# A hybrid decoder trunk on one core: the last up unit of a feed-forward window, made in two halves of 256 columns

## The chip, the cores and the metric

The kernel runs on one core of one Trainium2 chip. The metric is device time in microseconds (us) of one execution. Three runs of the kernel before took 2665.16, 2666.79 and 2670.24 us, so the median is 2666.79.

The engines are named as in the profile: PE (TensorE matmuls), PEld (its weight loads), DVE (VectorE), ACT (ScalarE), POOL (GpSimd) and SP (SyncE, which issues the DMAs). Each runs its own program in order, and they wait for each other through semaphores.

## The reference

The input x has 1024 tokens of 1024 features, in float32. Two layers follow each other, then a last RMSNorm. In each layer

```python
h = rmsnorm(x, norm_mix[l])
proj = h @ w_in[l]
mix = concat([s5_mixer(...), dsa_attention(...), retention(...)])   # all causal
x = x + mix @ w_out[l]
h = rmsnorm(x, norm_ffn[l])
gate, up = jnp.split(h @ w_ffn_in[l], 2, axis=-1)      # 2816 columns each
x = x + (jax.nn.silu(gate) * up) @ w_ffn_out[l]
```

The change lies in the last three lines, the feed-forward part.

## The kernel before, in words

**Tiling.** Features lie on the 128 partitions, tokens on the free axis. The tokens are worked through in two halves of 512 (h = 0, 1) in each of the two layers (l = 0, 1). A *unit* is one product of a 128-feature slice of weights with all of the input features for 512 tokens: 8 feature tiles of 128. Its result fills one PSUM bank of 512 columns. There are 408 units, numbered u in the order in which they run. They are grouped in *windows*: `proj` (18 units), `mixout` (8) and `ffn` (76).

**Three products for one.** To keep float32 accuracy with the faster float32r products, each operand is split into a rounded high part and the low remainder. A tile product is then hi x hi + hi x lo + lo x hi, so a unit of 8 tiles has 24 products of 512 columns on PE, first the 16 with the weights' high part, then the 8 with their low part.

**Weights.** For unit u SP loads the slice into `w_raw` (three buffers) when unit u - 3 is done. ACT makes `w_hi` from it (`prep`, L835; two buffers, so it waits until unit u - 2 is done), POOL makes `w_lo` as the difference (`weight_lo`, L724).

**The feed-forward window.** The 22 slices of gate and up come in four chunks (4, 6, 6 and 6), listed in `FFN`: in a chunk gate and up units alternate, then eight down units multiply the chunk's 4 or 6 activation tiles with `w_ffn_out` and DVE adds them to x (`add_x`, L1179). Behind each chunk but the last, the first gate unit of the next chunk stands between the last up unit and the first down unit. In the last chunk the last up unit (number 67 of the window) stands directly ahead of the first down unit (number 68).

**From an up unit to an activation tile.** DVE multiplies the unit's bank with the gate (`atmp`, L1319). ACT rounds the product to `a_hi` (L942), and POOL makes the remainder `a_lo` (L806). A down unit needs both. In its first unit PE begins with all tiles of the chunk but the last (two products for each of five tiles here), then waits on `a_lo_ready` for the last.

**The order on ACT and POOL.** At the step of a unit, ACT's program first has `prep` of the unit behind it and then the `a_hi` of the up unit before it; POOL's has `weight_lo` of the unit behind it and then `a_lo`. So at the first down unit ACT's order is: cast of the weights of the second down unit (which waits for the end of the up unit), then `a_hi`; POOL's is: `w_lo` of the second down unit (which waits for that cast), then `a_lo`.

**Banks.** PSUM has eight banks of 512 columns: A and B are used by the units in turn, C and D (two each), E and F by the mixers. Before PE writes into a bank it calls `take`, which waits for the semaphore that `leave` noted when the bank was last filled: that of the engine which reads it out.

**The order of everything** is one list, `PLAN`, which each engine walks through. The mixers' steps are woven between the units. The attention of the half that comes next runs inside an `ffn` window: layer l, half 1 in the window (l, 0), and layer 1, half 0 in the window (0, 1); the window (1, 1) has none. The attention ends with `attend_end`. In its step 0 PE fills bank E with the last block's values (and leaves it to `mat_ready`) and bank F with the row factors; then ACT copies F (L1040), and in step 1 DVE reads E and writes the block's output (`block_out`, L1381), which counts `mat_ready` up. In the windows (0, 0) and (1, 0) the plan has both steps between the gate unit 66 and the up unit 67; in the window (0, 1) step 0 stands ahead of unit 66 and step 1 behind it.

Of the kernel before, what the change touches and what calls it, by code (L numbers as in the profile page):

```python
# [10 lines left out]
ALU = mybir.AluOpType  # L11
ACTF = mybir.ActivationFunctionType
F32 = mybir.dt.float32
# [4 lines left out]
P = 128  # L18
T, D, DEPTH = 1024, 1024, 2
HALF = 512  # L20
KT = D // P
TT = HALF // P
NB = T // P
# [27 lines left out]
FFN = []  # L51
# [225 lines left out]
def deferred(kind, l, h):  # L277

    return (kind, l, h) == ("proj", 1, 1) or kind == "ffn" and (l, h) != (0, 1)
# [4 lines left out]
    return (2, 3, 4, 5, 6, 0, 1, 7) if l else (0, 1, 6, 7, 2, 3, 4, 5)  # L284


def unit_pieces(u):
    kind, _, _, i = UNIT[u]
    return 2 if kind == "proj" and i == U_VK else 1
# [70 lines left out]
def build_trunk(nc, x, w_in, w_out, norm_mix, a_re, a_im, log_dt, b_re, b_im, c_re, c_im, ssm_d, glu_w,  # L360
                glu_b, rel_bias, ret_gn, norm_ffn, w_ffn_in, w_ffn_out, norm_final, const, out, at):
    ctx = ExitStack()
    with ctx:
# [134 lines left out]
        def bank(group, a=0, b=None):  # L498
            first, n = GROUPS[group]
            return psum[:, first * 512 + a:first * 512 + (n * 512 if b is None else b)]  # L500
# [8 lines left out]
        def w_lo(u, n=1024):  # L509
            return low[:, u % 3, 0:n]  # L510
# [14 lines left out]
                 "gate_ready", "atmp_ready", "a_hi_ready", "a_lo_ready", "x_added", "x1_stored", "x_out0",  # L525
                 "x_out1", "x_in0", "x_in1", "xa_loaded", "q_moved", "final_loaded", "final_turned", "final_out",
                 "out_stored0", "out_stored1", "out_stored2", "act_chain", "dve_chain", "pool_chain",
                 "round_step"] + [f"xtok_loaded{t}" for t in range(NB)]
        sems = {n: ctx.enter_context(nc.semaphore(n)) for n in names}
        block = ctx.enter_context(nc.Block())  # L530

# [183 lines left out]
        @block.gpsimd  # L715
        def _(eng):
            st = Counts()

            def weight_lo(u):
                if u >= UNITS:  # L720
                    return
                n = unit_width(u)
                eng.wait_ge(sems["hi_ready"], u + 1)
                eng.tensor_tensor(w_lo(u, n), w_raw[:, u % 3, 0:n], w_hi[:, u % 2, 0:n].bitcast(F32),  # L724
                                  ALU.subtract).then_inc(sems["weights_ready"], 1)

            def tile_lo(k, src):

                n = st.add("h_hi_ready")
                if k % 2 == 0:  # L730
                    eng.wait_ge(sems["h_hi_ready"], n)
                    eng.tensor_tensor(h_lo[:, k, :], src, h_hi[:, k, :].bitcast(F32), ALU.subtract).then_inc(  # L732
                        sems["h_lo_pool"], 1)

            def add_square(m):
                n = st.add("square_ready")
                if 0 < m < KT - 1:
                    eng.wait_ge(sems["square_ready"], n)
                    if m > 1:
                        eng.wait_ge(sems["ssq_added"], st.now("ssq_added"))  # L740
                    eng.tensor_tensor(ssq[:, :], ssq[:, :], tmp[:, 2 + m % 2, :], ALU.add).then_inc(sems["ssq_added"], 1)
                    st.add("ssq_added")

            def masks(l, h, b, j):

                at_ = attention[l, h]
                nk, heads = NK[b], 2 * at_.pairs
                far = nk - 256
                if (l, h, b, j) == (0, 0, 0, 0):
                    eng.wait_ge(sems["const_loaded"], 16)  # L750
                    eng.wait_ge(sems["bias_loaded"], 16)
                    eng.wait_ge(sems["y_gated"], 1)
                    for g in range(2):
                        eng.wait_ge(sems[f"x_out{g}"], 16)
                if b >= 2 and j == 0:
                    eng.wait_ge(sems["mask_ready"], st.add("mask_ready"))
                if st.now("nmax_ready"):
                    eng.wait_ge(sems["nmax_ready"], st.now("nmax_ready"))
                st.add("nmax_ready", heads)
                if b < 2:  # L760
                    for n in range(heads):
                        win = bias_win[:, 2 * j + n, ::-1]
                        if b:
                            eng.tensor_copy(at_.mask(b, n, 0, P), win[:, 0:P])
                        eng.tensor_tensor(at_.mask(b, n, nk - P, nk), table("noncausal"), win[:, P:256], ALU.add).then_inc(
                            sems[f"mask{n % 2}_ready"], 1)
                    return
                if j == 0:
                    eng.tensor_copy(at_.near, score[b][:, far:nk]).then_inc(sems["pool_chain"], 1)
                    for n in range(1, heads):  # L770
                        eng.tensor_copy(at_.mask(b, n, 0, far), score[b][:, 0:far])
                    eng.wait_ge(sems["pool_chain"], st.add("pool_chain"))
                for n in range(heads):
                    eng.tensor_tensor(at_.mask(b, n, far, nk), at_.near, bias_win[:, 2 * j + n, ::-1], ALU.add).then_inc(
                        sems[f"mask{n % 2}_ready"], 1)

            for step in PLAN:
                what = step[0]
                if what == "fillnorm":
                    if step[2:4] == (0, 0):  # L780
                        weight_lo(0)
                    for k in range(KT):
                        tile_lo(k, fill_tmp(step[4], k))
                elif what == "fillraw" and step[2]:
                    st.add("h_hi_ready", KT)
                elif what == "fillmix":
                    for k in mix_order(step[1]):
                        tile_lo(k, mix_source(step[2], k))
                elif what in GEMMS:
                    kind, l, h, i, u = step  # L790
                    if i < GEMMS[kind]:
                        weight_lo(u + 1)
                    if kind == "mixout" and i:
                        add_square(i - 1)
                    if kind == "ffn" and i:
                        did, c, f = FFN[i - 1]
                        if did == "gate" and deferred(kind, l, h):
                            eng.wait_ge(sems["gate_ready"], st.add("gate_ready"))
                            eng.tensor_tensor(gate, gate, row, ALU.mult).then_inc(sems["gate_scaled"], 1)
                        elif did == "gate":  # L800
                            st.add("gate_ready")
                        if did == "up":
                            if (l, h, c, f) == (0, 0, 0, 0):
                                eng.wait_ge(sems["q_moved"], 16)
                            eng.wait_ge(sems["a_hi_ready"], st.add("a_hi_ready"))
                            eng.tensor_tensor(a_lo[:, f, :], atmp, a_hi[:, f, :].bitcast(F32), ALU.subtract).then_inc(  # L806
                                sems["a_lo_ready"], 1)
                        if did == "down" and c == LAST_CHUNK:
                            add_square(f)
                            if h == 0:  # L810
                                tile_lo(f, mix_source(1, f))
                            elif l == 0:
                                st.add("h_hi_ready")
                elif what == "attend":
                    _, l, h, b, j, s = step
                    if s == 0 and j == 0:
                        masks(l, h, b, 0)
                    elif s == 1 and j + step_pairs(l, h) < PAIRS:
                        masks(l, h, b, j + step_pairs(l, h))
# [3 lines left out]
        def _(eng):  # L823
# [100 lines left out]
            def ffn(l, h, i, u):  # L924
# [13 lines left out]
                    act(gate, scaled, ACTF.Silu).then_inc(sems["gate_ready"], 1)  # L938
                if did == "up":
                    st.add("a_lo_ready")  # L940
                    eng.wait_ge(sems["atmp_ready"], st.add("atmp_ready"))
                    act(a_hi[:, f, :], atmp, ACTF.Copy).then_inc(sems["a_hi_ready"], 1)  # L942
                if did == "down":
                    st.add("x_added")
                    if c == LAST_CHUNK:
# [221 lines left out]
        def _(eng):  # L1167
# [131 lines left out]
            def ffn(l, h, i, u):  # L1299
# [7 lines left out]
                        eng.wait_ge(sems["gate_ready"], st.now("gate_ready"))  # L1307
                    tt(scaled, bank(g), row, MUL).then_inc(sems["gated"], 1)  # L1308
                elif did == "up":
                    eng.wait_ge(sems["unit_done"], u)  # L1310
                    st.add("gate_ready")
                    if later:
                        eng.wait_ge(sems["gate_scaled"], st.add("gate_scaled"))
# [2 lines left out]
                    if st.now("a_lo_ready"):  # L1316
                        eng.wait_ge(sems["a_lo_ready"], st.now("a_lo_ready"))
                    st.add("a_lo_ready")
                    tt(atmp, bank(g), gate, MUL).then_inc(sems["atmp_ready"], 1)  # L1319
                elif did == "down":  # L1320
                    eng.wait_ge(sems["unit_done"], u)
                    add_x(f, g)
# [426 lines left out]
        def _(eng):  # L1749
# [11 lines left out]
            def take(*groups):  # L1761

                for g in groups:
                    first, n = GROUPS[g]
                    for b in range(first, first + n):
                        for sem, count in kept.pop(b, ()):
                            eng.wait_ge(sems[sem], count)
# [88 lines left out]
            def ffn(l, h, i, u):  # L1856
# [7 lines left out]
                g = unit_bank("ffn", i)  # L1864
                if what == "gate":
                    unit(g, u, "gated" if deferred("ffn", l, h) else "gate_ready")
                elif what == "up":
                    unit(g, u, "atmp_ready")
                else:
# [381 lines left out]
```

## Time and profile before

| | |
|---|---|
| runs, us | 2665.16, 2666.79, 2670.24 |
| span of the profiled execution, us | 2668.5 |
| time of the profiled execution beside its span | not listed |
| mean granted TensorE clock | 0.987 |
| busy: PE, PEld | 2551.4 us (96%), 2007.8 us (75%) |
| busy: DVE, POOL, ACT | 1553.0 us (58%), 1308.9 us (49%), 1020.3 us (38%) |
| DMA | 232.91 MB, 87 GB/s on average |

The profile shows one execution. A row of a group of instructions gives line, engine, operation, tiles as out<-in, shape and count, then the busy time in us and the mean duration of one in ns, then the engine's idle time before them and what ended it. A row of the timeline gives the start and the length in us, counted from the start of the span, and in brackets the idle time ahead of it and what ended that. The duration of a product runs from its start to its modelled end; products overlap, so their pace is read from their starts.

### The profile page before, as it was taken

The page shows a single profiled execution, that of the slowest core. Times are in us where ns is not written, and L with a number is a line of the kernel's source. Part 1 is how long each engine was busy: PE and PEld are TensorE (multiplying, and loading weights), DVE is VectorE, ACT ScalarE, POOL GpSimd, SP SyncE. Part 2 cuts the span into 40 slices and gives each one's busy share as a digit, 9 for nine tenths or more (in the row PEclk, how much of TensorE's full clock was granted, in tenths as well). Part 3 has the DMA queues.
Part 4 walks back from the last instruction along what each step waited for, and adds up shares of the span by engine and source line. Part 5 has one row for each costly group of instructions (what it writes and reads, how often), then busy time and mean ns, then how long its engine had stood idle before and what let it go on. Part 6 is the DMA issues. An engine that isn't in the chain of part 4 may idle for free.

```text
span 2668.5 us, 34623 instructions
## 1 busy us (share of the span) xinstructions
PE 2551.4 (96%) x13515; PEld 2007.8 (75%) x13515; DVE 1553.0 (58%) x2691; ACT 1020.3 (38%) x1478; POOL 1308.9 (49%) x818
## 2 busy tenths in 40 slices
PE   8998979999999999999999999999999999999998
PEld 6766757677777777778777787777777777888887
DVE  3769767799997226833331385677999922211111
ACT  5232354244435433324344422442534453322222
POOL 3332344455545564536555532544555447665654
PEclk9988999999999999999999999999999999999998
DMA  5341112132222153323322242222222215233332
GB/s 165 85 132 41 49 53 90 52 91 72 78 71 64 58 189 95 87 64 91 91 77 82 80 138 56 79 60 76 77 77 60 79 44 201 79 103 103 108 110 82
DMA packets 385666, 232.91 MB, mean 87 GB/s; under 512 B 29593, under 2 KB 371553, under 8 KB 383073
## 3 DMA queue, kind: packets, MB, share of 16 engines
q1 hardware_dynamic: 385136, 229.62, 29.0%
q8 instruction: 109, 1.79, 0.3%
q10 hardware_dynamic: 368, 1.08, 0.1%
q14 instruction: 53, 0.43, 0.0%
HBM read 213.88 MB, written 14.69 MB: 86 GB/s over the span
## 4 chain that ended last, share of the span: by engine, by line
PE 68%; DVE 25%; ACT 3%; issue 3%; POOL 1%; DMA 1%; DVEq 0%; ACTq 0%; SPq 0%
PE psum L1759 65%; DVE scores L1361 7%; DVE top L1359 7%; PE psum L2079 1%; DVE psum L1395 1%; DVE xs L1179 1%; DVE scores L1347 1%; DVE tmp L1319 1%; ACT w_hi L835 0%; ACT scratch L1036 0%; POOL w_lo L724 0%; DVE tmp L1308 0%; DVE scratch L1428 0%; PE psum L2176 0%; ACT xs L1054 0%
## 5 line engine op out<-in xcount | busy, mean ns | idle before, releaser
L724 POOL TENSOR_TENSOR w_lo<-w_raw,w_hi 128x1024 fp32r<-128x1024 f32 (+2 forms) x408 | 900.8, 2208 | 1197.9 <-ACT w_hi L835 1197.8
L1759 PE MATMUL psum<-h_hi,w_hi 128*128 128x512 f32 x1984 | 796.4, 401 | 15.2 <-ACT h_hi L859 7.4
L835 ACT ACTIVATE w_hi<-w_raw 128x1024 fp32r<-128x1024 f32 (+2 forms) x408 | 397.7, 975 | 1047.9 <-PE psum L1759 989.4
L1759 PE MATMUL psum<-h_lo,w_hi 128*128 128x512 f32 x1984 | 763.2, 391 | 0.9 <-POOL h_lo L732 0.9
L1759 PE MATMUL psum<-h_hi,w_lo 128*128 128x512 f32 x1984 | 514.4, 390 | 0.0
L1759 PEld LDWEIGHTS psum<-h_hi,w_hi 128*128 128x128 f32 x1984 | 374.9, 189 | 128.3 <-issue 36.1
L1759 PEld LDWEIGHTS psum<-h_lo,w_hi 128*128 128x128 f32 x1984 | 373.9, 189 | 78.3 <-issue 1.9
L1759 PEld LDWEIGHTS psum<-h_hi,w_lo 128*128 128x128 f32 x1984 | 373.3, 188 | 76.6
L1359 DVE MAX8 top<-scores 128x8 f32<-128x512 f32 (+5 forms) x352 | 324.3, 921 | 7.8
L1361 DVE MATCH_REPLACE8 scores<-top,scores 128x512 f32<-128x512 f32 (+5 forms) x352 | 319.0, 906 | 0.0
L1179 DVE TENSOR_TENSOR xs<-xs,psum 128x512 f32<-128x512 f32 x160 | 109.6, 686 | 315.0 <-PE psum L1759 304.5
L1759 PE MATMUL psum<-a_hi,w_hi 128*128 128x512 f32 x704 | 279.2, 397 | 7.2 <-POOL a_lo L806 7.2
L1759 PE MATMUL psum<-a_lo,w_hi 128*128 128x512 f32 x704 | 274.9, 390 | 0.0
L1319 DVE TENSOR_TENSOR tmp<-psum,tmp 128x512 f32<-128x512 f32 x88 | 60.8, 691 | 245.0 <-PE psum L1759 243.9
L1759 PE MATMUL psum<-a_hi,w_lo 128*128 128x512 f32 x704 | 182.7, 393 | 0.0
L1759 PEld LDWEIGHTS psum<-a_hi,w_hi 128*128 128x128 f32 x704 | 132.6, 188 | 41.9 <-POOL a_lo L806 8.9
L1759 PEld LDWEIGHTS psum<-a_hi,w_lo 128*128 128x128 f32 x704 | 133.5, 190 | 28.1
L1759 PEld LDWEIGHTS psum<-a_lo,w_hi 128*128 128x128 f32 x704 | 132.7, 188 | 26.5
L806 POOL TENSOR_TENSOR a_lo<-tmp,a_hi 128x512 fp32r<-128x512 f32 x88 | 116.9, 1329 | 30.8 <-ACT a_hi L942 30.8
L1308 DVE TENSOR_TENSOR tmp<-psum,tmp 128x512 f32<-128x512 f32 x66 | 45.6, 691 | 122.1 <-PE psum L1759 114.8
L1759 PE MATMUL psum<-w_hi,h_hi 128*128 128x512 f32 x256 | 102.8, 402 | 4.4 <-ACT iqT L905 4.3
L1759 PE MATMUL psum<-w_hi,h_lo 128*128 128x512 f32 x256 | 100.5, 393 | 0.0
(310 smaller groups left out, 2913.5 us busy)
## 6 DMA issues: line engine op xcount, KB each, us to landing
w_raw<-in_w_ffn_in_dram SPq DMA_DIRECT2D x176, 512.0 KB, 3.8
w_raw<-in_w_ffn_out_dram SPq DMA_DIRECT2D x96, 384.0 KB, 3.1
w_raw<-in_w_in_dram SPq DMA_DIRECT2D x68, 512.0 KB, 3.8
w_raw<-in_w_out_dram SPq DMA_DIRECT2D x32, 512.0 KB, 3.6
x_half<-xs SPq DMA_DIRECT2D x8, 1024.0 KB, 6.5
xs<-x_half SPq DMA_DIRECT2D x8, 1024.0 KB, 6.9
w_raw<-in_w_ffn_out_dram SPq DMA_DIRECT2D x32, 256.0 KB, 2.7
out_dram<-mixed SPq DMA_DIRECT2D x8, 512.0 KB, 4.5
```

Source lines behind the costliest of these rows:

```text
L724: eng.tensor_tensor(w_lo(u, n), w_raw[:, u % 3, 0:n], w_hi[:, u % 2, 0:n].bitcast(F32), ALU.subtract).then_inc(sems["weights_ready"], 1)
L806: eng.tensor_tensor(a_lo[:, f, :], atmp, a_hi[:, f, :].bitcast(F32), ALU.subtract).then_inc(sems["a_lo_ready"], 1)
L835: act(w_hi[:, u % 2, 0:n], w_raw[:, u % 3, 0:n], ACTF.Copy).then_inc(sems["hi_ready"], 1)
L1179: tt(xs[:, m, :], xs[:, m, :], bank(g), ADD).then_inc(sems["x_added"], 1)
L1308: tt(scaled, bank(g), row, MUL).then_inc(sems["gated"], 1)
L1319: tt(atmp, bank(g), gate, MUL).then_inc(sems["atmp_ready"], 1)
L1347: ins = stt(score[b], bank(g, 0, NK[b]), w, score[b], MUL, ADD)
L1359: eng.max(out=top8[:, :], in_=src).then_inc(sems["round_step"], 1)
L1361: eng.match_replace(out=src, in_to_replace=top8[:, :], in_values=src, imm_value=TAKEN).then_inc(sems["round_step"], 1)
L1395: eng.tensor_tensor_reduce(bank(g, 0, nk), bank(g, 0, nk), at_.mask(b, n), -1.0, 3e38, ADD, ALU.min, nmax[:, i:i + 1]).then_inc(sems["nmax ...
L1759: return eng.matmul(out_, lhsT, rhs, start=start, stop=stop, skip_group_check=True)
L2079: ins = eng.transpose(bank(g, k * P, (k + 1) * P), at_.prob[:, n, k * P:(k + 1) * P], ident)
```

## The change

The last up unit of each window is made in two halves of 256 columns. `halved(i)` is true where unit i is an up unit and unit i + 1 a down unit. PE makes columns 0 to 255 in bank E (all 24 products, each of 256 columns), counts `up_half` up, then makes columns 256 to 511 in the unit's own bank and counts `unit_done` up. DVE, ACT and POOL each make their step in two halves, with semaphores `atmp_half` and `a_hi_half` for the first half and the old ones for the second. PE takes both banks before its first product.

```diff
+def halved(i):
+    return 0 < i + 1 < len(FFN) and FFN[i][0] == "up" and FFN[i + 1][0] == "down"
...
 # POOL
+                            if halved(i - 1):
+                                eng.wait_ge(sems["a_hi_half"], st.add("a_hi_half"))
+                                eng.tensor_tensor(a_lo[:, f, 0:256], atmp[:, 0:256], a_hi[:, f, 0:256].bitcast(F32),
+                                                  ALU.subtract)
+                                eng.wait_ge(sems["a_hi_ready"], st.add("a_hi_ready"))
+                                eng.tensor_tensor(a_lo[:, f, 256:512], atmp[:, 256:512],
+                                                  a_hi[:, f, 256:512].bitcast(F32), ALU.subtract).then_inc(
+                                    sems["a_lo_ready"], 1)
...
 # ACT
+                    if halved(i - 1):
+                        eng.wait_ge(sems["atmp_half"], st.add("atmp_half"))
+                        act(a_hi[:, f, 0:256], atmp[:, 0:256], ACTF.Copy).then_inc(sems["a_hi_half"], 1)
+                        eng.wait_ge(sems["atmp_ready"], st.add("atmp_ready"))
+                        act(a_hi[:, f, 256:512], atmp[:, 256:512], ACTF.Copy).then_inc(sems["a_hi_ready"], 1)
...
 # DVE
+                    if halved(i - 1):
+                        eng.wait_ge(sems["up_half"], st.add("up_half"))
+                    else:
+                        eng.wait_ge(sems["unit_done"], u)
...
+                    if halved(i - 1):
+                        tt(atmp[:, 0:256], bank("E", 0, 256), gate[:, 0:256], MUL).then_inc(sems["atmp_half"], 1)
+                        eng.wait_ge(sems["unit_done"], u)
+                        tt(atmp[:, 256:512], bank(g, 256, 512), gate[:, 256:512], MUL).then_inc(sems["atmp_ready"], 1)
...
 # PE
+                elif halved(i):
+                    hi, lo = w_hi[:, u % 2, :], w_lo(u)
+                    eng.wait_ge(sems["hi_ready"], u + 1)
+                    take("E", g)
+                    for c0 in (0, 256):
+                        cols = slice(c0, c0 + 256)
+                        out_ = bank(g if c0 else "E", c0, c0 + 256)
+                        for k in range(KT):
+                            w = slice(k * P, (k + 1) * P)
+                            mm(out_, hi[:, w], h_hi[:, k, cols], k == 0, False)
+                            mm(out_, hi[:, w], h_lo[:, k, cols], False, False)
+                        eng.wait_ge(sems["weights_ready"], u + 1)
+                        for k in range(KT):
+                            ins = mm(out_, lo[:, k * P:(k + 1) * P], h_hi[:, k, cols], False, k == KT - 1)
+                        ins.then_inc(sems["unit_done" if c0 else "up_half"], 1)
+                    leave("E", "atmp_half")
+                    leave(g, "atmp_ready")
```

The semaphores `up_half`, `atmp_half` and `a_hi_half` are new. The other units are made as before.

## Rows read from the trace of the kernel before

**Rows 1.** The page: busy time of each engine; the chain that ended last, by engine.
```profile
PE 2551.4 (96%) x13515; PEld 2007.8 (75%) x13515; DVE 1553.0 (58%) x2691; ACT 1020.3 (38%) x1478; POOL 1308.9 (49%) x818
...
PE 68%; DVE 25%; ACT 3%; issue 3%; POOL 1%; DMA 1%; DVEq 0%; ACTq 0%; SPq 0%
```

**Rows 2.** The waits of PE: engine, line, waited for: us, times, longest us.
```profile
PE psum L1759 <- POOL a_lo L806: 7.2, 4, 1.8
```

**Rows 3.** The timeline around the end of the up unit, window (1, 1).
```profile
2613.51 1.98 PE L1759 MATMUL psum<-h_hi,w_lo 128*128 128x512 f32 x8
2615.33 0.39 PE L1759 MATMUL psum<-a_hi,w_hi 128*128 128x512 f32 x1
2615.53 0.69 DVE L1319 TENSOR_TENSOR tmp<-psum,tmp 128x512 f32<-128x512 f32 x1 [4.75 <-PE psum L1759]
2615.53 0.85 ACT L835 ACTIVATE w_hi<-w_raw 128x768 fp32r<-128x768 f32 x1 [4.07 <-PE psum L1759]
...
2616.28 0.61 ACT L942 ACTIVATE a_hi<-tmp 128x512 fp32r<-128x512 f32 x1
2616.45 1.83 POOL L724 TENSOR_TENSOR w_lo<-w_raw,w_hi 128x768 fp32r<-128x768 f32 x1 [2.35 <-ACT w_hi L835]
...
2617.37 0.39 PE L1759 MATMUL psum<-a_lo,w_hi 128*128 128x512 f32 x1
2618.24 1.26 POOL L806 TENSOR_TENSOR a_lo<-tmp,a_hi 128x512 fp32r<-128x512 f32 x1
2619.55 0.50 PE L1759 MATMUL psum<-a_hi,w_hi 128*128 128x512 f32 x1 [1.80 <-POOL a_lo L806]
```

**Rows 4.** The group of POOL that makes the activations' low parts.
```profile
L806 POOL TENSOR_TENSOR a_lo<-tmp,a_hi 128x512 fp32r<-128x512 f32 x88 | 116.9, 1329 | 30.8 <-ACT a_hi L942 30.8
```

**Rows 5.** The timeline of POOL: a pair of operations on 256 columns.
```profile
1460.01 0.74 POOL L774 TENSOR_TENSOR scores<-scratch,bias_win 128x256 f32<-128x256 f32 x1
1460.70 0.74 POOL L774 TENSOR_TENSOR scratch<-scratch,bias_win 128x256 f32<-128x256 f32 x1
```

**Rows 6.** Groups of DVE and ACT by shape: 256 columns out of PSUM.
```profile
L1447 DVE TENSOR_TENSOR scratch<-psum,cst 128x256 f32<-128x256 f32 x32 | 12.0, 418 | 32.4 <-PE psum L1759 32.4
L1078 ACT ACTIVATE scratch<-psum 128x256 f32<-128x256 f32 x16 | 6.0, 377 | 39.6 <-PE psum L1759 39.6
```

**Rows 7.** Groups of PE by shape: 4-byte products of 512 and 256 columns.
```profile
L1759 PE MATMUL psum<-uy,area 128*128 128x512 f32 x48 | 23.3, 594 | 0.9 <-ACT scratch L1014 0.9
...
L1759 PE MATMUL psum<-uy,area 128*128 128x256 f32 x16 | 4.8, 379 | 0.0
```

**Rows 8.** 128 columns per weight: group of PE, timeline, group of weight loads.
```profile
L1759 PE MATMUL psum<-s_ct,scores 128*128 128x128 f32 x64 | 7.5, 275 | 0.0
...
204.07 3.73 PE L1759 MATMUL psum<-s_ct,scores 128*128 128x128 f32 x32
...
L1759 PEld LDWEIGHTS psum<-h_hi,w_hi 128*128 128x128 f32 x1984 | 374.9, 189 | 128.3 <-issue 36.1 <-ACT h_hi L859 8.4 <-ACT w_hi L835 4.2
```

**Rows 9.** The timeline ahead of the up unit, windows (0, 0) and (0, 1).
```profile
904.37 0.48 PE L1759 MATMUL psum<-h_hi,w_hi 128*128 128x512 f32 x1
904.65 0.60 ACT L1040 ACTIVATE scratch<-psum 128x512 f32<-128x512 f32 x1 [7.89 <-PE psum L1759]
905.28 0.69 DVE L1381 TENSOR_TENSOR mixed<-psum,scratch 128x512 f32<-128x512 f32 x1 [11.13 <-ACT scratch L1040]
...
1486.23 0.69 DVE L1381 TENSOR_TENSOR mixed<-psum,scratch 128x512 f32<-128x512 f32 x1 [2.05 <-ACT scratch L1040]
...
1490.87 0.39 PE L1759 MATMUL psum<-h_hi,w_hi 128*128 128x512 f32 x1
```

**Rows 10.** Stretches from PE's restart to the third down unit, with granted clock.
```profile
914.15:920.22 6.07, 6.07 (x27) 4.99 (x27) 0.69 (x1) 1.89 (x3) 2.97 (x2) 1.00 0.23 67
1500.53:1508.15 7.62, 7.62 (x26) 6.16 (x27) 2.51 (x2) 1.98 (x3) 1.84 (x1) 0.78 0.17 52
2205.03:2211.09 6.06, 6.06 (x26) 4.99 (x27) 0.69 (x1) 1.89 (x3) 2.96 (x2) 1.00 0.23 68
2619.55:2627.19 7.64, 7.64 (x26) 6.13 (x27) 0.69 (x1) 1.36 (x2) 1.84 (x1) 0.78 0.18 54
```

More of the change, by code:

```diff
@@ L527, in build_trunk @@
                  "out_stored0", "out_stored1", "out_stored2", "act_chain", "dve_chain", "pool_chain",
-                 "round_step"] + [f"xtok_loaded{t}" for t in range(NB)]
+                 "round_step", "up_half", "atmp_half", "a_hi_half"] + [f"xtok_loaded{t}" for t in range(NB)]
         sems = {n: ctx.enter_context(nc.semaphore(n)) for n in names}
@@ L804, in _ @@
                                 eng.wait_ge(sems["q_moved"], 16)
-                            eng.wait_ge(sems["a_hi_ready"], st.add("a_hi_ready"))
-                            eng.tensor_tensor(a_lo[:, f, :], atmp, a_hi[:, f, :].bitcast(F32), ALU.subtract).then_inc(
-                                sems["a_lo_ready"], 1)
+                            if halved(i - 1):
[7 more added lines that the diff above has]
+                            else:
+                                eng.wait_ge(sems["a_hi_ready"], st.add("a_hi_ready"))
+                                eng.tensor_tensor(a_lo[:, f, :], atmp, a_hi[:, f, :].bitcast(F32), ALU.subtract).then_inc(
+                                    sems["a_lo_ready"], 1)
                         if did == "down" and c == LAST_CHUNK:
@@ L940, in ffn @@
                     st.add("a_lo_ready")
-                    eng.wait_ge(sems["atmp_ready"], st.add("atmp_ready"))
-                    act(a_hi[:, f, :], atmp, ACTF.Copy).then_inc(sems["a_hi_ready"], 1)
+                    if halved(i - 1):
[3 more added lines that the diff above has]
+                        act(a_hi[:, f, 256:512], atmp[:, 256:512], ACTF.Copy).then_inc(sems["a_hi_ready"], 1)
+                    else:
+                        eng.wait_ge(sems["atmp_ready"], st.add("atmp_ready"))
+                        act(a_hi[:, f, :], atmp, ACTF.Copy).then_inc(sems["a_hi_ready"], 1)
                 if did == "down":
@@ L1309, in ffn @@
                 elif did == "up":
-                    eng.wait_ge(sems["unit_done"], u)
+                    if halved(i - 1):
+                        eng.wait_ge(sems["up_half"], st.add("up_half"))
+                    else:
+                        eng.wait_ge(sems["unit_done"], u)
                     st.add("gate_ready")
@@ L1318, in ffn @@
                     st.add("a_lo_ready")
-                    tt(atmp, bank(g), gate, MUL).then_inc(sems["atmp_ready"], 1)
+                    if halved(i - 1):
+                        tt(atmp[:, 0:256], bank("E", 0, 256), gate[:, 0:256], MUL).then_inc(sems["atmp_half"], 1)
+                        eng.wait_ge(sems["unit_done"], u)
+                        tt(atmp[:, 256:512], bank(g, 256, 512), gate[:, 256:512], MUL).then_inc(sems["atmp_ready"], 1)
+                    else:
+                        tt(atmp, bank(g), gate, MUL).then_inc(sems["atmp_ready"], 1)
                 elif did == "down":
```

## The prediction

> **What bounds the kernel now.** I read the page first: TensorE (PE) is busy for 96% of the span, and in the chain that ended last PE has 68% and VectorE (DVE) 25% [rows 1]. So a microsecond counts if PE stands still for it or spends it on products. Next I read PE's own waits, because the change sits between the last up unit of a feed-forward window and its first down unit: PE waited for POOL's a_lo (L806) 4 times, 7.2 us in all, 1.8 us the longest [rows 2]. Four windows, four waits: that is the place, and 7.2 us is all that stands there.
>
> The timeline of the last of the four shows what ends the wait [rows 3]. The up unit's last products start at 2613.51 (eight in 1.98 us); the first down unit begins at 2615.33 without a gap. The up result is seen by the other engines at 2615.53: DVE multiplies it with the gate (0.69), and ACT begins the cast of the next down unit's weights (L835, 0.85), which waits for the same result and stands ahead of a_hi in ACT's program. a_hi follows at 2616.28 and is done at 2616.89. POOL starts at 2616.45, when the cast ends, with the low part of those weights (L724, 1.83), and only then makes a_lo (2618.24, 1.26, so to 2619.50). PE goes on at 2619.55. The reader is to see that a_hi lay ready for 2618.24 - 2616.89 = 1.35 us before POOL took it up. The late chain is cast, w_lo, a_lo; the product and a_hi are not on it.
>
> **The change, part by part.** It acts on one unit in each of the four windows: only in the last chunk does an up unit stand directly ahead of a down unit.
>
> *The halved chain.* DVE can make its first half once half the unit is done. But ACT's first half of a_hi is still written behind the cast, which waits for the whole unit, and POOL's first half of a_lo behind w_lo, which waits for that cast. Nothing on the late chain starts earlier. The half products and casts are hidden: a DVE operation on 256 columns from PSUM takes 0.42, one of ACT 0.38 [rows 6], so the second product ends by 2615.53 + 0.42 = 2615.95 and two casts from 2616.28 on end by 2617.04, still 1.2 us ahead of POOL. Without that cover, what exceeds 1.2 us would add to the stall. DVE's new wait holds only its own second half and the later additions to x, ACT's comes after the cast and is met by then; behind POOL's waits stands the w_lo of a later unit. SyncE's weight loads wait on the unit's end as before.
>
> What is left is that POOL makes two operations of one. A pair on 256 columns: the second starts 0.69 after the first and takes 0.74, together 1.43 [rows 5], against 1.26 in place [rows 3], hence +0.17 (the mean of all a_lo, 1.33, holds slower ones [rows 4]). From below, halves that cost exactly half add 0; from above, 2 x 0.74 and a pause of 0.07 as between cast and w_lo [rows 3] make 1.55, +0.29. I take the pair, as the nearest row: 4 x 0.17 = +0.7 us (0 to 1.2).
>
> *Half-width products.* 24 products of 512 columns become 48 of 256, each with a weight load of its own. The 512-column pace is (1.98 - 0.39)/7 = 0.227 us [rows 3]. No product in this number format is narrower in the trace, so I bound it. If the pace is proportional to the columns, 256 cost 0.1135 and the unit is unchanged. The 4-byte products at their slower rate fall from 594 to 379 ns between 512 and 256 columns, 0.84 ns a column [rows 7]; half of that is 0.42 for this format, whose 512 columns would be 0.215, which leaves 0.012 fixed per product: 0.107 + 0.012 = 0.119 then, and 48 x 0.119 - 24 x 0.227 = +0.27 us a unit. Above that stands the row of rival B. I take 0.118, nearer the fixed end, because it is what differs between the two formats: +0.22 a unit, +0.9 us in all (0 to 1.1).
>
> Does a weight load hide behind a product this short? Products on 128 columns with a new 128x128 weight each ran 32 in 3.73 us, that is (3.73 - 0.275)/31 = 0.111 apart, though a load is listed with 189 ns [rows 8]: loads overlap with the stream and with one another. So 0.118 isn't held up by them. The Trainium skill (TensorE: Matmul & The Clock Gate, "Measured speedup vs the span model") says instead that a weight load overlaps with running matmuls only where the row group differs, and all loads here use every row. By that rule and the page's figure for a load of 128 columns (section "LDWEIGHTS", about 107 ns) the 24 added loads of a unit would show, an estimate of 2.6 us a unit and 10 us in all. The rows above speak against it.
>
> *A second bank.* This is the largest term. The first half goes to bank E, so PE must now wait, before the unit's first product, for whoever last used E. In the feed-forward windows that carry the attention of a second half (two of four, one in each layer), PE's last attention step stands directly ahead of this very up unit: it fills E (the weighted values) and F, and E is free only when DVE has made the block's output (L1381), which needs ACT's copy of F (L1040). In the trace PE starts the unit at 904.37, while ACT's copy runs from 904.65 and L1381 from 905.28 to 905.97 [rows 9]. With 0.05 from DVE's end to PE's start, as behind a_lo [rows 3], the unit starts at 906.02: +1.65 us. Everything behind it on PE moves by that; nothing takes it back, since the gate's chain ended before the unit did and down products follow. The other such window has the same rows some 1291 us later. In layer 0's second window E is free at 1486.23 + 0.69 = 1486.92 and the unit starts at 1490.87 [rows 9]: no wait. The fourth has no attention. So 2 x 1.65 = +3.3 us (to 3.5 with a weight load of 0.1 shown after each pause).
>
> *The clock.* Two of the four stalls of 1.8 us are followed by the lower level. From PE's restart to the third down unit takes 6.07 and 6.06 us at a granted clock of 1.00, and 7.62 and 7.64 at 0.78, where PE ran partly at 1.2 instead of 2.4 GHz [rows 10]. So a fall costs 1.6 us. A slightly longer stall and two new pauses can bring one more fall, shifted times one fewer; I put 0 into the sum and -1.6 to +3.2 into the range.
>
> **The sum.** 0.7 + 0.9 + 3.3 = +4.9 us. The profiled execution has a span of 2668.5 (no time of its own is listed beside that), 1.7 above the median of the runs, 2666.79. On the span it gives 2673.4; on the median, the figure that will be compared, 2671.7.
>
> **Rivals.**
> A. *Faster: the early half frees the end of POOL's chain.* Place: POOL between the unit's end and a_lo. If the first halves of a_hi and a_lo were done before w_lo, or a_lo were bound by a_hi, the stall would shrink and the clock would hold: at most 4 x 1.8 + 2 x 1.6 = 10.4 gained against 0.9 + 3.3 paid, 6.2 us faster, 2660.6. It decides in favour of the change once each stall is below 1.8 - 4.2/4 = 0.75 us. For it speaks only that the second half is all that needs the end of the unit; against it, that a_hi now waits 1.35 us for POOL [rows 3].
> B. *Weight loads show at half width.* The 24 added loads at the 189 ns listed [rows 8] are 4.5 us a unit, 18.1 in all, and with 0.7 + 3.3 that makes 22 us: 2688.9. For it: no 256-column product of this format has been seen. Against it: 0.111 apart at 128 columns.
> C. *No wait for bank E*, because E is released early enough or PE is late there anyway: 0.7 + 0.9 = +1.6 us, 2668.4. For it: only two instances, and an order of steps that I read from the plan. Against it: 904.37 is 1.6 us before L1381's end.
> D. *The clock falls more often*, twice to three times net: 4.9 + 3.2 to 4.8, 8.1 to 9.7 us: 2674.9 to 2676.5. For it: the two falls after stalls of 1.8 us; against it, the two stalls without one.
> That the change does not do what it says (an early chain that is not early) is already the forecast's first part.
>
> **How the numbers follow.** Forecast 0.64, A 0.05, B 0.07, C 0.12, D 0.12. 0.2% of the median is 5.3 us, about what a measurement of this kernel can tell from no change. The forecast's 4.9 lies just inside, and by its own bounds (0 + 0 + 3.3 to 1.2 + 1.1 + 3.5, and one fall either way) it goes 0.36 to "same" and 0.28 to slower. A goes to faster, C to "same", B and D to slower: faster 0.05, same 0.48, slower 0.47. The range reaches from below C to the upper end of D, 2667.8 to 2677.0, and leaves out A, B and tails.
>
> **What would show it.** PE's four waits for a_lo at 1.9 to 2.1 us, not shorter; the a_lo group with four more operations, eight of them on 256 columns, the first right behind w_lo; 48 products in 5.6 to 5.75 us without gaps; PE idle before the up unit of the first and third windows by 1.4 to 1.7 us, released by DVE L1381. It would be wrong if the a_lo waits fall below 1.5 us, if the half products stand over 0.13 apart, or if no wait for E appears.

## The result: slower by 0.3 to 0.5 per cent

The changed kernel took 2680.55 us in the median of four runs (2679.74 to 2684.52); the kernel before, in four runs, 2665.97. The ratio is 1.0049 with a 95% interval from 1.0034 to 1.0064. Measured again later beside 31 runs of the kernel before, the ratio was 1.0030 (1.0019 to 1.0041), which is 8.0 us (5 to 11) of 2670. So the change makes the kernel slower, by more than the 4.9 us forecast, though the lower end of the second interval is only just above it. The predicted range, 2667.8 to 2677.0, did not hold the time.

The profiled execution has a span of 2678.0 us, 9.5 more than that of before. The page and, below it, PE's waits (us in all, times, longest), to be read against [rows 1, 2]:

```profile
PE 2558.5 (96%) x13611; PEld 2017.6 (75%) x13611; DVE 1554.0 (58%) x2695; ACT 1020.7 (38%) x1482; POOL 1309.9 (49%) x822
...
PE 68%; DVE 23%; ACT 3%; issue 3%; POOL 2%; DMA 1%; SPq 0%; DVEq 0%; ACTq 0%; POOLq 0%
```

PE's waits:

```profile
PE psum L1787 <- POOL a_lo L815: 7.7, 4, 1.9
PE psum L1787 <- ACT w_hi L849: 2.9, 2, 1.5
```

PE waits for a_lo as often as before and 0.5 us longer in all; and a row is new, 2.9 us in two waits. PE has 96 more products, 24 in each of four units.

The timeline of the first window, in order of time (start, length, engine, line):

```profile
904.78 0.60 ACT L1060 ACTIVATE scratch<-psum 128x512 f32<-128x512 f32 x1 [7.91 <-PE psum L1787]
905.27 0.83 ACT L849 ACTIVATE w_hi<-w_raw 128x768 fp32r<-128x768 f32 x1
905.41 0.69 DVE L1409 TENSOR_TENSOR mixed<-psum,scratch 128x512 f32<-128x512 f32 x1 [11.14 <-ACT scratch L1060]
...
906.20 0.36 PE L1787 MATMUL psum<-h_hi,w_hi 128*128 128x256 f32 x1 [1.46 <-ACT w_hi L849]
...
908.19 1.12 PE L1787 MATMUL psum<-h_hi,w_lo 128*128 128x256 f32 x8
...
909.52 0.42 DVE L1343 TENSOR_TENSOR tmp<-psum,tmp 128x256 f32<-128x256 f32 x1 [2.82 <-PE psum L1787]
...
912.03 0.40 PE L1787 MATMUL psum<-a_hi,w_hi 128*128 128x512 f32 x1
912.23 0.85 ACT L849 ACTIVATE w_hi<-w_raw 128x768 fp32r<-128x768 f32 x1 [4.18 <-PE psum L1787]
...
912.98 0.40 ACT L957 ACTIVATE a_hi<-tmp 128x256 fp32r<-128x256 f32 x1
913.15 1.83 POOL L729 TENSOR_TENSOR w_lo<-w_raw,w_hi 128x768 fp32r<-128x768 f32 x1 [3.73 <-ACT w_hi L849]
...
913.29 0.40 ACT L959 ACTIVATE a_hi<-tmp 128x256 fp32r<-128x256 f32 x1
...
914.94 0.72 POOL L812 TENSOR_TENSOR a_lo<-tmp,a_hi 128x256 fp32r<-128x256 f32 x1
915.62 0.72 POOL L815 TENSOR_TENSOR a_lo<-tmp,a_hi 128x256 fp32r<-128x256 f32 x1
916.40 0.50 PE L1787 MATMUL psum<-a_hi,w_hi 128*128 128x512 f32 x1 [1.92 <-POOL a_lo L815]
```

Three things are to be seen. DVE has its first half at 909.94, but ACT's first a_hi begins at 912.98, behind the cast that waited for the whole unit, and POOL's first a_lo only behind w_lo. The half ran ahead on DVE alone. Next, the up unit starts at 906.20, just behind the end of DVE's block output (905.41 + 0.69 = 906.10); before it started ahead of that operation [rows 9]. The row names ACT's w_hi as releaser, since that cast also ends at 906.10; it is a cast for the down unit, which the up unit doesn't need. Such a label goes by the times alone, and the code decides; e2 below settles it. Last, the half products stand (1.12 - 0.28)/7 = 0.120 us apart.

Then the clock. The stretches from PE's restart to the third down unit, as [rows 10] (length, PE, PEld, DVE, ACT and POOL busy, granted clock, DMA):

```profile
916.40:924.03 7.63, 7.63 (x27) 6.12 (x27) 0.69 (x1) 1.88 (x3) 3.09 (x2) 0.78 0.17 52
1507.36:1515.01 7.65, 7.65 (x27) 6.13 (x27) 2.51 (x2) 1.98 (x3) 1.85 (x1) 0.78 0.18 54
2213.93:2221.58 7.65, 7.65 (x27) 6.12 (x27) 0.69 (x1) 1.89 (x3) 3.10 (x2) 0.78 0.17 51
2630.66:2638.27 7.61, 7.61 (x26) 6.13 (x27) 0.69 (x1) 1.37 (x2) 1.84 (x1) 0.78 0.17 52
```

All four are at 0.78 now; before, the first and the third were at 1.00. That is two more falls at 1.57 us.

**Where the 9.5 us of the spans went.** In window (0, 0) ACT's copy of F starts at 904.65 before and 904.78 after, the third down unit at 920.22 and 924.03: 3.68 us more in between, of which 1.7 is the later start of the unit, 0.28 its width, 0.12 the stall and 1.56 the clock. Window (1, 0) gives 3.71 in the same way, (0, 1) 0.50 and (1, 1) 0.43, where only width and stall add. Together 8.3 us; the other 1.2 lie in stretches that the change does not touch, where falls of the clock come at other times (between 964 and 1034 us the granted clock is 0.95, and between 960 and 1030 of before it was 1.00; between 205 and 240 it is 0.85, and 0.80 before).

### The profile page after: what moved, and what is told of

Read it like the earlier page. It is cut to its first block, busy times and chain, and to the rows that moved or that the text cites. A ratio compares the mean times of both kernels' runs of the same rounds, so it can differ in the third digit from the quotient of the medians.

```text
span 2678.0 us, 34827 instructions
## 1 busy us (share of the span) xinstructions
PE 2558.5 (96%) x13611; PEld 2017.6 (75%) x13611; DVE 1554.0 (58%) x2695; ACT 1020.7 (38%) x1482; POOL 1309.9 (49%) x822
## 4 chain that ended last, share of the span: by engine, by line
PE 68%; DVE 23%; ACT 3%; issue 3%; POOL 2%; DMA 1%; SPq 0%; DVEq 0%; ACTq 0%; POOLq 0%
PE psum L1787 66%; DVE scores L1389 7%; DVE top L1387 7%; DVE psum L1423 1%; PE psum L2124 1%; POOL w_lo L729 1%; DVE xs L1199 1%; DVE scores L1375 1%; DVE tmp L1347 1%; ACT w_hi L849 0%; ACT scratch L1056 0%; DMA w_raw<-in_w_out_dram 0%; DVE scratch L1456 0%; POOL h_lo L737 0%; PE psum L1949 0%
## 5 line engine op out<-in xcount | busy, mean ns | idle before, releaser
L1787 PE MATMUL psum<-h_hi,w_hi 128*128 128x512 f32 (+1 forms) x2016 | 801.5, 399 | 16.9 <-ACT h_hi L873 6.5
L1787 PE MATMUL psum<-h_lo,w_hi 128*128 128x512 f32 (+1 forms) x2016 | 767.7, 389 | 0.9 <-POOL h_lo L737 0.9
L1787 PE MATMUL psum<-h_hi,w_lo 128*128 128x512 f32 (+1 forms) x2016 | 516.3, 387 | 0.0
L1787 PEld LDWEIGHTS psum<-h_hi,w_hi 128*128 128x128 f32 x2016 | 382.3, 190 | 129.3 <-issue 36.1
L1787 PEld LDWEIGHTS psum<-h_lo,w_hi 128*128 128x128 f32 x2016 | 380.8, 189 | 77.4 <-issue 1.9
```

The source lines that it names most:

```text
L1787: return eng.matmul(out_, lhsT, rhs, start=start, stop=stop, skip_group_check=True)
```

## The experiments

All were timed in five rounds beside the kernel before. In e4, e5, e9 and e12 the added products go into a bank that nothing reads. Microseconds are the ratio's distance from 1 times 2670, with its interval. The measured medians of the kernel before stood at 2670.57, 2669.41, 2670.43 and 2670.53 (31, 22, 29 and 15 runs; single runs from 2662.55 to 2678.34).

| run | edit | us against before |
|---|---|---|
| e1 | the changed kernel | +8.0 (5.1 to 10.9) |
| e2 | e1, first half in bank C0 | +3.2 (0.8 to 5.9) |
| e3 | before, wait for bank E alone | +6.1 (3.2 to 9.1) |
| e6 | before, half-width products alone | +1.6 (-1.1 to 4.3) |
| e11 | before, halved chain alone | +3.5 (0.8 to 5.9) |
| e4 | e1, stall filled | +5.6 (2.9 to 8.3) |
| e5 | before, stall filled | -2.9 (-5.3 to -0.5) |
| e9 | e3, stall filled | +2.4 (-0.5 to 5.1) |
| e12 | e4, pauses filled too | +4.5 (1.9 to 7.5) |
| e7 | before, POOL's order swapped | -7.7 (-11.2 to -4.5) |
| e8 | e2, early order on ACT and POOL | -10.4 (-13.6 to -6.9) |
| e10 | e8 with bank E | -4.8 (-7.7 to -2.1) |

**The change again, and its parts.**

> The changed kernel once more, beside the kernel before on the same chip. Theory 1 (the direct terms of about 5.1 us, which the two profiles show, plus more falls of the clock behind the longer stall and the new pauses): 11 to 16 us slower than before, in all rounds. Theory 2 (direct terms alone; the first comparison had a slow sample): 4 to 7 us slower.

8.0 us by the ratio and 9.4 by the medians (2679.96 against 2670.57). That is between the two theories: the interval, 5.1 to 10.9, takes in the upper part of theory 2's 4 to 7 and ends just below theory 1's 11. This run alone does not part them.

> As the changed kernel, but the first half goes to the first bank of group C in place of bank E, so PE need not wait for the attention's output. Theory 1: the two pauses of 1.46 us (1.7 us of delay each) ahead of the up unit go, 3.4 us, and with them any fall of the clock that they bring: 3.4 to 7 us faster than the changed kernel, so 7 to 12 us slower than before. Theory 2: exactly 3.4 us faster than the changed kernel. The stall for a_lo stays at 1.92 us in all four windows under both.

```diff
-                    take("E", g)
+                    take("C0", g)
...
-                    leave("E", "atmp_half")
+                    leave("C0", "atmp_half")
```

With bank C0 the new waits are gone (no row of them is left in PE's waits, so the label w_hi stood for bank E), and 4.8 us of the 8.0 with them. That difference of two ratios is uncertain by 3.9. Set directly against e1, timed in the same rounds, the twelve runs of e2 are 5.5 us faster in the mean, with an uncertainty of 1.6: more than the 3.4 of direct delay, as theory 1 has it. Theory 1 had put e2 at 7 to 12 us slower than before; it is 3.2, as e1 too came out lower than it said. The profile shows a place for what exceeds the delay; the four stretches of this run:

```profile
914.53:920.57 6.04, 6.04 (x27) 4.99 (x27) 0.69 (x1) 1.89 (x3) 2.96 (x2) 1.00 0.22 65
1503.55:1511.17 7.62, 7.62 (x27) 6.12 (x28) 2.52 (x2) 1.98 (x3) 1.86 (x1) 0.78 0.18 54
2208.35:2214.38 6.03, 6.03 (x27) 4.99 (x27) 0.69 (x1) 1.89 (x3) 2.96 (x2) 1.00 0.22 65
2623.56:2631.16 7.60, 7.60 (x27) 6.15 (x27) 0.69 (x1) 1.37 (x2) 1.84 (x1) 0.78 0.17 52
```

The stall is still 1.92 us, and yet the first and third stretch are at full clock again.

> The kernel before with one edit: PE waits for bank E ahead of the last up unit, which is made whole in its own bank as before. Theory 1: two pauses of 1.46 us appear, 2 x 1.65 to 1.7 = 3.3 to 3.4 us directly, and up to 4 us more from the clock: 3 to 8 us slower than before. Theory 2: 3.3 to 3.4 us slower.

```diff
+                    if i + 1 < len(FFN) and FFN[i + 1][0] == "down":
+                        take("E")
                     unit(g, u, "atmp_ready")
```

The wait alone costs 6.1 us, near twice its direct delay of 3.4, which lies just inside the interval (3.2 to 9.1). Here the trace names its releaser rightly, and in one of the two windows that have the pause the clock falls behind the stall that follows. PE's waits:

```profile
PE psum L1759 <- POOL a_lo L806: 7.2, 4, 1.8
PE psum L1759 <- DVE mixed L1381: 2.8, 2, 1.4
```

Its first and third stretch from the restart to the third down unit:

```profile
917.61:925.28 7.67, 7.67 (x27) 6.14 (x28) 0.69 (x1) 1.88 (x3) 3.10 (x2) 0.78 0.18 53
...
2214.12:2220.19 6.07, 6.07 (x27) 4.99 (x27) 0.69 (x1) 1.89 (x3) 2.97 (x2) 1.00 0.23 67
```

Seven profiles together have a pattern. In the windows (0, 0) and (1, 0) the stall for a_lo was followed by the lower level in 5 of 6 cases with the pause ahead of the unit (the changed kernel twice over, e3) and in 0 of 8 without it (before, e2, e6, e11). In the other two windows, where the change adds no pause, it was 12 of 14 in the same seven profiles. Each profile is one execution, though; what all runs say of it stands behind e11.

> The kernel before with one edit: the last up unit of each window is made as 48 products of 256 columns, both halves in the unit's own bank; the products, casts and low parts behind it are whole as before. Direct term by the changed kernel's profile: 4 x 0.31 = 1.2 us. Theory 1: 0.5 to 3 us slower than before, with the stall for a_lo at 1.80 us. The rival, that the added weight loads show, would give 10 us or more.

```diff
+                    for c0 in (0, 256):
+                        cols = slice(c0, c0 + 256)
+                        out_ = bank(g, c0, c0 + 256)
...
+                    ins.then_inc(sems["unit_done"], 1)
```

1.6 us, with 1.2 expected from the width. The interval holds 0, but not the 10 us of loads that show.

> The kernel before with one edit: product, a_hi and a_lo behind the last up unit are made in halves of 256 columns, while PE makes the unit whole in its own bank. Direct term: POOL's two operations end 0.12 us later, 4 x 0.12 = 0.5 us, stall 1.92 us. Theory 1: 0 to 2.5 us slower than before. If halving by itself shortened the chain, it would be faster.

```diff
-                    if halved(i - 1):
-                        eng.wait_ge(sems["up_half"], st.add("up_half"))
-                    else:
-                        eng.wait_ge(sems["unit_done"], u)
+                    eng.wait_ge(sems["unit_done"], u)
...
-                        tt(atmp[:, 0:256], bank("E", 0, 256), gate[:, 0:256], MUL).then_inc(sems["atmp_half"], 1)
+                        tt(atmp[:, 0:256], bank(g, 0, 256), gate[:, 0:256], MUL).then_inc(sems["atmp_half"], 1)
...
-                elif halved(i):
+                elif False:
```

Halving the chain does not shorten it: PE's stall is 1.94 us in all four windows. 3.5 us (0.8 to 5.9) is more than the 0.5 of direct cost and above the 2.5 expected at most, which the interval still takes in. Its profiled execution does not show the excess: there only one of four stalls is followed by the lower level.

The mean granted clock is listed for every run, however, and shows what a single profile cannot. If time at 1.2 GHz costs half of itself against 2.4 GHz, a mean clock that is lower by 0.001 costs 2.67 us of 2670. This is an estimate, uncertain by 1.5 to 3 us in each row and rather too high, since time at the lower level counts in it whether PE works or not:

| run | mean clock of its runs | of before's runs beside it | cost of the difference, us | with the direct term, us | measured, us |
|---|---|---|---|---|---|
| e1 | 0.9851 (8 runs) | 0.9869 (31) | 4.8 | 4.8 + 5.1 = 9.9 | 8.0 |
| e2, no pause | 0.9859 (12) | 0.9869 (31) | 2.6 | 2.6 + 1.7 = 4.3 | 3.2 |
| e3, the pause alone | 0.9858 (12) | 0.9869 (31) | 2.9 | 2.9 + 3.4 = 6.3 | 6.1 |
| e6, no pause | 0.9864 (11) | 0.9871 (22) | 1.9 | 1.9 + 1.2 = 3.1 | 1.6 |
| e11, no pause | 0.9852 (12) | 0.9870 (29) | 5.0 | 5.0 + 0.5 = 5.5 | 3.5 |

Each sum lies inside the interval of its measurement. So the excess of e11 fits time at the lower level, in executions other than the profiled one; no trace shows where. And by this estimate e11, without any pause, loses as much to the clock as the changed kernel does. A pause ahead of the unit is therefore not needed for a lower clock, and the pattern of the seven profiles does not show that the pause is the cause.

**The clock.**

> The changed kernel, with eight more products of 512 columns on PE ahead of each wait for the last a_lo of the chunk (8 x 0.227 = 1.8 us of work in a spare bank that nothing reads), so that PE is busy through the stall of 1.92 us and nothing else is moved. Theory 1 (the clock falls behind the stall): the four falls behind it go, 3 to 6.4 us faster than the changed kernel although PE does more work. Theory 2 (the clock has no part): the same time as the changed kernel or up to 0.5 us slower.

> The kernel before with the same eight spare products of 512 columns ahead of each of the four waits for the last a_lo, 8 x 0.227 = 1.82 us of work in place of 1.80 us of standing still. Theory 1 (the clock falls behind some of these stalls, at 1.6 us each): 1.5 to 3.5 us faster than before; and the filled changed kernel then stands about 5.1 us, the direct terms, behind this one. Theory 2 (falls behind these stalls cost nothing): the same as before or up to 0.5 us slower.

```diff
                         if f == 0 and k == n - 1:
+                            if c == LAST_CHUNK:
+                                take("C0")
+                                for _ in range(8):
+                                    mm(bank("C0"), hi[:, 0:P], a_hi[:, 0, :], True, True)
                             eng.wait_ge(sems["a_lo_ready"], made)
```

PE works for the 1.8 us it would stand still, nothing else becomes earlier, and the kernel before gets 2.9 us faster; the changed kernel's median drops by 3.4 us, from 2679.96 to 2676.57. In both profiles the granted clock behind all four stalls is 1.00. For e5 the gain agrees with two falls at the 1.57 us that [rows 10] give, and theory 2 is out: a stall had a second price that is paid after it. For e4 it is only half of four falls, 6.3 us, though the mean granted clock of its runs, 0.9874 against 0.9851 of e1, would be worth some 6 us by the estimate above; why no more came back is not explained. The two filled kernels stand 8.5 us apart, with an uncertainty of 3.6, so the 5.1 expected is possible.

> The kernel before with PE's wait for bank E (as in e3) and the eight spare products in the stall for a_lo (as in e5). Theory 1 (the wait for E costs its 3.3 us and, beyond that, only falls of the clock behind the a_lo stalls that follow it): 3 to 4.5 us slower than e5, so 0 to 2 us slower than before. Theory 3 (the pauses ahead of the up unit bring falls of their own): 5 to 7 us slower than e5, so 2 to 4.5 us slower than before.

> As e8 (both halves early on ACT and POOL, no stall for a_lo), but with the first half in bank E as the change has it. Theory 1: e8 and the wait for E alone, 3.4 us: 5 to 6.5 us faster than before. Theory 3: 5 to 7 us slower than e8, so 2 to 4.5 us faster than before. Both say that with the order on ACT and POOL mended the change would have made the kernel faster, bank E and all.

> The changed kernel as in e4 (eight spare products in each stall for a_lo) with six more (6 x 0.227 = 1.36 us, into a spare bank) in each pause of 1.46 us ahead of the up unit. The direct terms stay (5.1 us). Theory 1 (the pauses matter only through the stall that follows, which is filled here): the same as e4, some 5 to 6 us slower than before. Theory 3 (the pauses bring falls of their own): 1.5 to 3.5 us faster than e4, so 2 to 4 us slower than before, which would be e5 (2.9 faster than before) plus the direct terms.

```diff
+                    if h == 0:
+                        take("C0")
+                        for _ in range(6):
+                            mm(bank("C0"), hi[:, 0:P], h_hi[:, 0, :], True, True)
                     take("E", g)
```

These three ask whether the pauses cost more than their delay where no stall follows. e9 is 5.3 us behind e5 (theory 1 says 3 to 4.5, theory 3 says 5 to 7), e10 5.6 behind e8 (3.4, or 5 to 7), and e12 1.1 ahead of e4 (0, or 1.5 to 3.5); the uncertainty of each difference is about 4. They are inconclusive: the first two lean to falls of their own, the third to none. One thing that both theories said of e10 did come: with the order on ACT and POOL mended, the change is 4.8 us faster than before (2.1 to 7.7), bank E and all.

**What the halves could have done.**

> The kernel before with one edit: at the first down unit of the last chunk POOL makes a_lo ahead of the next unit's w_lo. If POOL's order sets the stall, as the rows of before say (a_hi lies ready for 1.35 us), a_lo ends 1.25 us earlier and the stall falls from 1.80 to about 0.55 us: 4 x 1.25 = 5 us, with the falls of the clock behind the stall gone up to 8.5 us faster than before. If the product and the cast of a_hi set the stall, it stays near 1.8 us and the time is that of before.

```diff
+                    swapped = kind == "ffn" and 0 < i < len(FFN) and FFN[i - 1][0] == "up" and FFN[i][0] == "down"
-                    if i < GEMMS[kind]:
+                    if i < GEMMS[kind] and not swapped:
                         weight_lo(u + 1)
...
+                        if swapped:
+                            weight_lo(u + 1)
```

The four waits for a_lo fall from 7.2 to 2.2 us, as POOL takes a_hi up at once. PE's wait, and then the timeline of the fourth window, against [rows 3]:

```profile
PE psum L1762 <- POOL a_lo L807: 2.2, 4, 0.6
```

```profile
2612.71 0.61 ACT L945 ACTIVATE a_hi<-tmp 128x512 fp32r<-128x512 f32 x1
...
2613.40 1.28 POOL L807 TENSOR_TENSOR a_lo<-tmp,a_hi 128x512 fp32r<-128x512 f32 x1 [2.87 <-ACT a_hi L945]
...
2614.64 1.85 POOL L724 TENSOR_TENSOR w_lo<-w_raw,w_hi 128x768 fp32r<-128x768 f32 x1
2614.74 0.50 PE L1762 MATMUL psum<-a_hi,w_hi 128*128 128x512 f32 x1 [0.55 <-POOL a_lo L807]
```

That is 5.0 us of waiting; the measured 7.7 (4.5 to 11.2) leaves room for the falls that went with it, but does not show them. In the profile the granted clock is 1.00 behind all four stalls, yet over all runs it averages 0.9872 against 0.9871 beside it.

> The changed kernel with bank C0 in place of E, and with both halves of a_hi ahead of the cast of the next weights on ACT and both halves of a_lo ahead of w_lo on POOL, so that the first half can run ahead. After the unit's end only 0.42 + 0.40 + 0.72 us and three hand-overs remain, against 2.27 us of products on PE: no stall. 4 x 1.80 = 7.2 us gained, 1.2 us paid for the width, and up to 3.2 us from the clock: 6 to 9 us faster than before. If the halves bring nothing by themselves beyond POOL's order, it is no faster than e7.

```diff
 # ACT, with the same swap on POOL as in e7
-                if i < len(FFN):
+                if i < len(FFN) and not (i and halved(i - 1)):
                     prep(u + 1)
...
                         act(a_hi[:, f, 256:512], atmp[:, 256:512], ACTF.Copy).then_inc(sems["a_hi_ready"], 1)
+                        prep(u + 1)
```

PE no longer waits for a_lo at all. POOL and the product that needs its result, first window:

```profile
909.95 0.74 POOL L813 TENSOR_TENSOR a_lo<-tmp,a_hi 128x256 fp32r<-128x256 f32 x1 [1.05 <-ACT a_hi L960]
910.97 0.74 POOL L816 TENSOR_TENSOR a_lo<-tmp,a_hi 128x256 fp32r<-128x256 f32 x1 [0.28 <-ACT a_hi L962]
...
912.11 0.39 PE L1791 MATMUL psum<-a_hi,w_hi 128*128 128x512 f32 x1
```

The second a_lo is done at 911.71, 0.4 us before PE comes to it. 2660.13 us in the median is 0.39% (0.26 to 0.51) faster than before, and this is the fastest kernel of this study, 18 us below the changed one by the ratios, with the same products. The 6 to 9 us expected lie for the most part inside the interval, 6.9 to 13.6.

## Why the prediction was wrong

Point by point, by its own steps:

- *The halved chain.* Right. Nothing on the late chain started earlier; the stall grew from 1.80 to 1.92, +0.12 where +0.17 was taken. e7 and e8 show the reason given, the order on ACT and POOL, from the other side.
- *Half-width products.* Right in the pace: 0.120 us apart against 0.118 taken and 0.119 for the fixed end. The term was somewhat small: without a pause the unit takes 5.75 to 5.76 us instead of 5.44, so 1.2 us in all where 0.9 was taken and 1.1 was the bound. Rival B falls, by this and by e6: the loads do not show. The Trainium skill (TensorE: Matmul & The Clock Gate, "The mechanism", the section ahead of the one that the prediction names) states that a load overlaps with running products only where the row group differs. By that rule the unit would have taken 2.6 us more, by the prediction's estimate from the page's figure for a load; the trace does not agree, with 0.3 us more.
- *A second bank.* Right in place, cause and direct size: two pauses, 1.7 us of delay each for 1.65 predicted, none in the other windows. Rival C falls. Rival A does too, for the change as it is; e8 is what A described, with the first halves done ahead of w_lo, and gains 10.4 us.
- *The sum of the direct terms*, 4.9 us, is 5.1 in the profile: 2 x 1.7 + 4 x 0.31 + 4 x 0.12.
- *The clock.* This is the step that failed: "I put 0 into the sum". The prediction named the longer stall and the new pauses as what could bring a fall, and then let shifted times cancel it, without a row for that. Nothing cancelled. The profiled execution has two falls more behind the stalls, 3.1 us, in the two windows with the pause, and over all runs the listed clock puts the cost at some 4.8 us. In the profile of e2 the stall is as long, 1.92 us, and the clock held in those two windows, so there the difference is the pause some 10 us ahead; but e11 has no pause and a mean clock as low. Which part of the change brings the falls is not shown. Rival D, two falls more, is what the trace shows; I gave it 0.12.
- *The base.* The sum was put on the median of three runs, 2666.79. The kernel before later had medians of 2669.4 to 2670.6 over 97 runs. With that base D's price, 8.1 us, meets the remeasured 8.0 and the changed kernel's medians of 2679.96 and 2680.55 are 9 to 11 above. The three runs spread over 5 us, as much as the effect, and the profiled span of 2668.5 was a sign that the base was low: the changed kernel's profiled execution took 2679.9 for a span of 2678.0, so before's would have been near 2670.4, which fits the slowest of the three, 2670.24. The median of the 97 is 2670.3, so the base was 3.5 us low; with 5.1 of direct terms and 4.8 of clock it gives 2680.2, against 2679.96 and 2680.55 measured. Of the 14.6 us of the first comparison, then, some 5 are direct, some 5 are the clock, and 4.3 are the low first runs of before; that last part is argued from the later medians, not shown. The low base weighs as much in the missed range as the clock does: moved up by 3.5 us, the range would have ended at 2680.5.

What stays open: which part of the change lets the clock fall. Each of the three parts alone went with a lower mean clock, by an estimate of 1.9 to 5.0 us, but those estimates are uncertain by up to 3 us and add up to more than the whole change lost. Whether the pauses act by what they do to PE or by moving the stalls in time is not shown either.

## What to carry to other kernels

Splitting a producer's work shortens a chain only if each later engine can take up the first half: look in the program order of every engine on the chain for what stands ahead of it, and first try that order (a few lines gave 7.7 us here, where the split alone cost 8). A spare bank is free only if its last reader is done by the time that PE comes to it; compare the reader's end with PE's start in every window. And where PE's idle time changes anywhere, price the granted clock behind each stall nearby; check it against the clock listed for all runs, since one profile is one execution. Take the base from more runs the smaller the effect is: here three runs put it 3.5 us low, for an effect of 8.

## What the hardware showed unexpectedly

Making PE do useless work made the program faster: eight products nobody reads, in each of four stalls of 1.8 us, gained 2.9 us (0.5 to 5.3), since behind these stalls the granted clock then stayed at the upper level of 2.4 GHz (1.00 behind all four in the profile, where two had 0.78).
